# Opening of a two-model block kernel: weights brought in tile by tile, silu on one row, and a reordered softmax in layer 0

## The reference, cut to what matters

```python
c_act = jax.nn.silu(c)                              # one row of 1024
for l in range(DEPTH):                              # 2
    mod = c_act @ ada_w[l] + ada_b[l]               # 1024 x 6144
    shift_m, scale_m, gate_m, shift_f, scale_f, gate_f = split(mod, 6)
    h = rms_norm(x, g_pre_mix[l]) * (1.0 + scale_m) + shift_m
    proj = h @ w_in[l] + b_in[l]                    # 1024 x 1280
    q, k, v, u = split(proj)                        # rotary on q and k
    attn_out = sliding_window_attention_with_sinks(q, k, v, sinks[l])
    pool_out = causal_pool_mixer(u, pool_w[l], pool_scale[l])
    mix = concatenate([attn_out, pool_out]) @ w_out[l]
    x = x + gate_m * rms_norm(mix, g_post_mix[l])
    h = rms_norm(x, g_pre_ffn[l]) * (1.0 + scale_f) + shift_f
    f = (silu(h @ w_gate[l]) * (h @ w_up[l])) @ w_down[l]
    x = x + gate_f * rms_norm(f, g_post_ffn[l])
```

## Time and profile before

| what | value |
|---|---|
| runs, median of 3 | 1170.61 us (1170.38 to 1171.25) |
| profiled execution, its own time | 1170.48 us |
| span in that profile | 1168.5 us |
| PE busy | 1140.9 us, 98% of the span |
| PE weight loads | 1020.5 us, 87% |
| DVE busy | 811.5 us, 69% |
| ACT busy | 628.0 us, 54% |
| granted TensorE clock | 0.999 |
| moved by DMA | 254.04 MB, mean 217 GB/s |

### The profile page before, as it was taken

The page is one execution under the profiler, slowest core; times in us unless marked ns, Lnnn a source line. Parts: engine busy times, 40 slices in busy tenths (PEclk is TensorE's granted clock), DMA queues, the critical chain, the costliest instruction groups (busy, mean ns, idle before and its releaser), DMA issues.

```text
span 1168.5 us, 19588 instructions
## 1 busy us (share of the span) xinstructions
PE 1140.9 (98%) x7862; PEld 1020.5 (87%) x7862; DVE 811.5 (69%) x1258; ACT 628.0 (54%) x1113; POOL 29.0 (2%) x68
## 2 busy tenths in 40 slices
PE   7999999999999999999999999999999999999997
PEld 4556999999887999999899899999989889999996
DVE  6698988776998756645677667656656866766653
ACT  3077544445566544445666766445556676655443
POOL 3100000000000000000000000000000000000000
PEclk9999999999999999999999999999999999999999
DMA  9995998887445866556343546555534435555530
GB/s 361 413 378 220 355 365 329 319 334 268 189 164 198 319 231 225 210 190 238 128 181 109 180 174 217 180 183 183 187 139 156 145 132 195 196 186 194 181 109 37
DMA packets 37996, 254.04 MB, mean 217 GB/s; under 512 B 4537, under 2 KB 4881, under 8 KB 9874
## 3 DMA queue, kind: packets, MB, share of 16 engines
q1 hardware_dynamic: 35138, 243.95, 56.6%
q0 software_dynamic: 2624, 8.84, 2.1%
q10 hardware_dynamic: 144, 0.00, 0.0%
HBM read 251.69 MB, written 1.08 MB: 216 GB/s over the span
## 4 chain that ended last, share of the span: by engine, by line
PE 86%; DVE 6%; ACT 3%; DMA 3%; issue 1%; SPq 0%; DVEq 0%; ACTq 0%
PE bank L497 26%; PE bank L499 25%; PE bank L498 25%; PE bank L504 3%; DMA raw_w<-weights 2%; DVE raw_w L1641 2%; PE bank L546 2%; PE bank L595 2%; ACT gtok L1173 1%; DVE lo_w L1628 1%; DMA shared<-bias_rows 1%; PE bank L946 1%; DVE tok L1853 0%; PE bank L638 0%; PE bank L897 0%
## 5 line engine op out<-in xcount | busy, mean ns | idle before, releaser
L1628 DVE TENSOR_TENSOR lo_w<-raw_w,hi_w 128x1024 fp32r<-128x1024 f32 (+3 forms) x346 | 409.4, 1209 | 122.7 <-ACT hi_w L1168 122.3
L1168 ACT ACTIVATE hi_w<-raw_w 128x1024 fp32r<-128x1024 f32 (+3 forms) x346 | 350.6, 1040 | 103.9 <-PE bank L499 89.2
L497 PE MATMUL bank<-in_hi,lo_w 128*128 128x256 f32 x1408 | 396.0, 281 | 0.0
L499 PE MATMUL bank<-in_hi,hi_w 128*128 128x256 f32 x1408 | 392.8, 279 | 0.0
L498 PE MATMUL bank<-in_lo,hi_w 128*128 128x256 f32 x1408 | 392.8, 279 | 0.0
L497 PEld LDWEIGHTS bank<-in_hi,lo_w 128*128 128x128 f32 x1408 | 264.3, 188 | 2.6 <-issue 0.8
L498 PEld LDWEIGHTS bank<-in_lo,hi_w 128*128 128x128 f32 x1408 | 263.7, 187 | 1.9 <-issue 0.5
L499 PEld LDWEIGHTS bank<-in_hi,hi_w 128*128 128x128 f32 x1408 | 264.7, 188 | 0.0
L497 PE MATMUL bank<-hi_w,hid_lo 128*128 128x512 f32 x352 | 139.6, 396 | 0.2 <-DVE hid_lo L2116 0.2
L498 PE MATMUL bank<-lo_w,hid_hi 128*128 128x512 f32 x352 | 139.0, 395 | 0.0
L499 PE MATMUL bank<-hi_w,hid_hi 128*128 128x512 f32 x352 | 139.0, 395 | 0.0
(11 more groups left out here) (227 smaller groups left out, 1141.1 us busy)
## 6 DMA issues: line engine op xcount, KB each, us to landing
raw_w<-weights SPq DMA_DIRECT2D x213, 1024.0 KB, 4.9
ink<-ink_w SPq DMA_DIRECT2D x8, 640.0 KB, 13.9
rows<-mod_rows POOLq DMA_DIRECT2D x7, 512.0 KB, 6.9
rows<-norm_rows POOLq DMA_DIRECT2D x5, 512.0 KB, 4.9
raw_w<-weights SPq DMA_DIRECT2D x4, 512.0 KB, 8.9
ink<-whole_w SPq DMA_DIRECT2D x2, 1024.0 KB, 22.2
early_out<-whole_w SPq DMA_DIRECT2D x2, 1024.0 KB, 7.6
raw_w<-weights SPq DMA_DIRECT2D x2, 832.0 KB, 4.5
```

Of the source, the lines that this page charges most:

```text
L497: nc.tensor.matmul(o, st[1], mv[0], start=start, stop=False, **kw)
L499: return nc.tensor.matmul(o, st[0], mv[0], start=False, stop=stop, **kw)
L1168: nc.scalar.activation(hi_w[:, m % NSPLIT, cut], raw_view(unit)[:, cut], ACT.Identity).then_inc(*sig("hi_w", unit, i))
L1628: nc.vector.tensor_tensor(lo_w[:, m % NSPLIT, cut], raw_view(unit)[:, cut], hi_w[:, m % NSPLIT, cut].bitcast(F32), ALU.subtract).then_inc( ...
```

## The change

SP brings the first eight ada units (which give shift and scale) by halves of 512 KB, tile by tile: both halves of tile t, then `ink[t]`. Before, only the first two units came by halves. The vectors come ahead of them. Tiles 0, 2, 4 and 6 (the even halves) signal four new semaphores, the odd ones the ring's own. DVE goes by single tiles where it went by pairs. Silu is applied by ACT to the one row before PE spreads it, and PE's vectors and norm turns are all ahead of the first product, with the vector copy in between on DVE. The bias load waits for ada unit 5 in place of 7. In layer 0's softmax ada unit 8 moves from before the last two evacuations to after `over_sum(0)`, and every later unit one place on; ACT's `shares(3)` and `shares(4)` go ahead of `exps(4)` and `exps(5)`. Banks are taken in another order, so that the first scores don't ask for the bank of the last place.

```diff
-INK_AFTER = {("ada", 0, 0): (1,), ("ada", 0, 1): (2,), ("ada", 0, 6): (3,), ("ada", 0, 2): (4,), ("ada", 0, 7): (5,),
-             ("ada", 0, 3): (6, 7)}
+TILE_IN = (0, 1, 2, 2, 0, 0, 1, 1)
...
-                    banks(4, 5, 6, 7, 2, 3)
+                    banks(5, 6, 7, 2, 3, 4)
...
-                    banks(0, 1, 4, 0, 1, *((6, 5, 7, 4) * 4))
+                    banks(0, 1, 5, 0, 1, *((7, 6, 5, 4) * 4))
...
-            pe.wait_ge(*due("c_in", 0))
+            pe.wait_ge(*due("c_act", "row"))
             for c in range(2):
                 job = ("opening", "c", c)
                 nc.tensor.matmul(take(job)[:, :], tmp[0:1, 0:P], c_row[0:1, cols(c)], start=True, stop=True).then_inc(*sig(*job))
             pe.wait_ge(*due("const_in", 0))
-            for T in range(2):
-                turn_norm(("mix", 0), T)
             pe.wait_ge(*due("vec_in", 0))
             transposes(("opening", "vec"), [vrow[:, P * g:P * (g + 1)] for g in range(NVEC)])
+            for c in range(2):
+                for T in range(2):
+                    turn_norm(("mix", 0), T, (c,))
...
+            def tiles_in(t, name):
+                j, f = t // 2, t % 2
+                for n in (2 * j, 2 * j + 1):
+                    if n >= NRAW and f == 0:
+                        sp.wait_ge(*due("ada", UNITS[n - NRAW][0]))
+                    src = a_w[size * n:size * (n + 1)].rearrange("(p f w) -> p f w", p=P, f=2)[:, f, :]
+                    sp.dma_start(raw_w[:, n % NRAW, D * f:D * (f + 1)], src).then_inc(*sig(name(n), t, n, by=16))
+
+            for t in range(KT):
+                tiles_in(t, (lambda n: f"tile_in{TILE_IN[n]}") if t % 2 == 0 else (lambda n: f"raw_w{n % NRAW}"))
+                sp.dma_start(ink[t], a_ink[t, :, :]).then_inc(*sig(f"ink_in{t}", by=16))
...
             angles()
+            pool.wait_ge(*due("ada", ("ada", 0, 5)))
+            load(bias, a_bias[0:1, :], 1280, "bias_in", 0)
             pool.wait_ge(*due("ada", ("ada", 0, 7)))
-            load(bias, a_bias[0:1, :], 1280, "bias_in", 0)
...
+            sc.preload_act_table_set("silu_and_others")
+
+            sc.wait_ge(*due("c_in", 0))
+            nc.scalar.activation(c_row[0:1, :], c_row[0:1, :], ACT.Silu).then_inc(*sig("c_act", "row"))
             sc.preload_act_table_set("natural_log_exp_and_others")
...
                 nc.scalar.activation(r, r, ACT.Exp, scale=-0.5).then_inc(*sig("rstd", N, 1))
-                sc.preload_act_table_set("silu_and_others")
 
                 sc.wait_ge(*due("opening", "c", 1))
                 for c in range(2):
-                    nc.scalar.activation(c_row[:, cols(c)], ps(("opening", "c", c))[:, :], ACT.Silu).then_inc(*sig("c_act", c, frees=("opening", "c", c)))
+                    copy(("opening", "c", c), c_row[:, cols(c)], ps(("opening", "c", c))[:, :], "c_act", c)
...
                     exps(3)
                     probT_in(0)
+                    shares(3)
                     exps(4)
-                    shares(3)
                     probT_in(1)
+                    shares(4)
                     exps(5)
-                    shares(4)
                     probT_in(2)
...
                 for T in range(2):
-                    norm(N, T)
-                ve.wait_ge(*due("c_act", 1))
-                ada_tile(0, 4, 0)
-                ada_tile(0, 0, 0)
+                    norm(N, T, (0,))
                 ve.wait_ge(*due("opening", "vec"))
                 nc.vector.tensor_copy(vcol[:, :], ps(("opening", "vec"))[:, 0:NVEC * P]).then_inc(*sig("vcol", 0, frees=("opening", "vec")))
+                for T in range(2):
+                    norm(N, T, (1,))
+                ve.wait_ge(*due("c_act", 1))
...
+                for t in range(KT):
+                    j, f = t // 2, t % 2
+                    ada_tile(0, 4 + j, f)
+                    last = ada_tile(0, j, f)
...
-                    ada(0, 8)
                     evacuate(0, 0, 2)
                     evacuate(0, 1, 2)
...
                     over_sum(0)
-                    ada(0, 9)
+                    ada(0, 8)
                     over_sum(1)
                     scored(2)
-                    ada(0, 10)
+                    ada(0, 9)
                     over_sum(2)
...
-                    for n in (18, 19, 12, 13, 14, 15):
+                    for n in (17, 18, 19, 12, 13, 14, 15):
```

More of the change, by code:

```diff
@@ L1031, in _ @@
                     sp.wait_ge(*due(*(("ada", old) if old[0] == "ada" else ("lo_w", old, 1))))
-                part, src = ((raw_w[:, n, D:2 * D], tiles[n][:, 1, :]) if n < 2 else
-                             (raw_view(unit), a_w[off:off + P * kt * n_cols].rearrange("(p w) -> p w", p=P)))
-                sp.dma_start(part, src).then_inc(*sig(f"raw_w{n % NRAW}", unit, by=16))
+                sp.dma_start(raw_view(unit), a_w[off:off + P * kt * n_cols].rearrange("(p w) -> p w", p=P)).then_inc(
+                    *sig(f"raw_w{n % NRAW}", unit, by=16))
                 off += P * kt * n_cols
@@ L1038, in _ @@
                     sp.dma_start(whole[u].rearrange("p t c -> p (t c)"), a_whole[u, :, :]).then_inc(*sig(f"whole_in{u}", by=16))
-                for kk in INK_AFTER.get(unit, ()):
-                    sp.dma_start(ink[kk], a_ink[kk, :, :]).then_inc(*sig(f"ink_in{kk}", by=16))
             for T in range(2):
@@ L1703, in scale, with norm @@
                     nc.vector.tensor_tensor(scaled[:, cols(c)], x[:, T, cols(c)], rows[:, 1, cols(c)], ALU.mult).then_inc(*sig("scaled", N, T, c))
-            def norm(N, T):
+            def norm(N, T, parts=(0, 1)):
                 ve.wait_ge(*due("rstd", N, 1 if N == ("mix", 0) else T))
                 r = tok_rstd[:, T, 1:2]
-                for c in range(2):
+                for c in parts:
                     dst = final[:, T, cols(c)] if N[0] == "final" else normed[:, cols(c)]
@@ L1835, in started @@
                         ve.wait_ge(*due("ada", ("ada", 0, j)))
                     ve.wait_ge(*due("vcol", 0))
-                    mod_column(0, "shift", 0, 0, a, b, shift[:, a:b])
-                    step(mod_column(0, "scale", 0, 8, a, b, scale[:, a:b]))
-                    for t in tiles:
-                        for T in range(2):
-                            ve.wait_ge(*due("turned", T, t // 4))
-                        nc.vector.tensor_scalar(raw[:, t, :], raw[:, t, :], scale[:, t:t + 1], shift[:, t:t + 1], ALU.mult, ALU.add).then_inc(
-                            *sig("scaled0", t))
+                    mod_column(0, "shift", 0, 0, t, t + 1, shift[:, t:t + 1])
@@ L1845, in in_job @@
+                    step(mod_column(0, "scale", 0, 8, t, t + 1, scale[:, t:t + 1]))
+                    for T in range(2):
+                        ve.wait_ge(*due("turned", T, t // 4))
+                    nc.vector.tensor_scalar(raw[:, t, :], raw[:, t, :], scale[:, t:t + 1], shift[:, t:t + 1], ALU.mult, ALU.add).then_inc(*sig("scaled0", t))
             def in_job(L, T, c):
@@ L2001, in attention_mixed @@
                 if L == 2:
-                    ve.wait_ge(*due("const_late", 0))
+                    ve.wait_ge(*due("const_in", 2))
                 ve.wait_ge(*due("crow_in", L))
```

51 lines of the change are left out of this document (23 added, 28 removed).

## The result

The changed kernel takes 1173.03 us at the median of 17 runs (1170.98 to 1174.64), the kernel before 1170.83 (1170.04 to 1171.51, 17 runs on the same chip). The ratio is 1.0018, with a 95% interval of 1.0012 to 1.0025: it is slower, by about 2.1 us. The forecast was 1170.3 in a range of 1168.0 to 1172.2; the time lies 0.8 above that range. The profiled execution took 1171.84 with a span of 1170.0, so it is one of the shorter ones, and what it shows is less than the whole loss.

The account below looks back on a forecast made before the run. The prediction took the boundary after layer 0's attention, waiting for the landing of `gu` 0 behind a full transfer queue, as the bound. It summed -0.7 (boundary) and +0.5 (landing) to -0.2 us: 1170.3, range 1168.0 to 1172.2.

Parts of the forecast that it names:

- the scores wait for no evacuation: Layer 0's attention: the first scores' wait of 1.67 us for DVE's last evacuation goes; they start at about 53.7.
- a wait for modcol ahead of the second row: PE, near 81 us: being early, it waits 1 to 2 us for the second modcol row it spreads.
- the shares worth nothing: Layer 0's softmax: PE's wait of 1.41 us at 74.14 goes, but PE then waits for modcol instead.
- the landing: Transfer of `gu` 0, landing at 92.9 before: 0.5 us lost, bounds 0 to 1.9, because later units are issued later.
- the upper bound: Transfer queue: each unit lands 5.5 us after its issue, unit 15 at 77.3 against 75.4, so 1.9 us lost.
- The gain of DVE in front is given back by the unit moved: DVE after `over_sum(5)`: there at 75.6 for 77.57, but at 77.9 with the seventh unit; last needed modcol at 92.0 to 92.3.
- 0.7 gained: Boundary after layer 0's attention: PE's turn of the norm ends at 102.65 us in place of 103.35.
- The turn: PE's turn of the boundary's norm: first half forecast to start at 101.35 us, before at 102.31.
- the norm's wait: DVE at the boundary: the norm's wait of 0.53 us shrinks by some 0.35, to 100.65.
- both waits of TensorE (near 41, and near 81): PE waits 2 to 3 us for `raw` late in the tiles and 1 to 2 us for modcol.
- Rival C: First transfer window: halves go at 377 in place of 420 GB/s, all lands 3.5 later; +2.8 us, 1173.3; chance 0.11.
- the prediction's own sign of being wrong: Boundary: `gu` 0 lands below 91 or above 95.9 us, or the boundary no longer waits for it.

Follow-up runs that it names:

- e7: The kernel before with only the shares ahead of the exps and the two new lists of banks: 1169.36 us, ratio 0.9985.
- e5: The kernel before with all of the softmax edits (unit 8 moved, shares, banks) and the old opening: 1171.01 us, ratio 1.0003.
- e1: The changed kernel with ada unit 8 put back ahead of the last two evacuations: 1171.35 us, ratio 1.0006.
- e8: The kernel before with the new opening alone; unit 8, shares and banks as before: 1173.32 us, ratio 1.0013.
- e11: The changed kernel with unit 8 put back and unread TensorE products ahead of tiles 6 and 7: 1169.94 us, ratio 0.9985.
- e13: The kernel before with the new opening alone and unread TensorE products ahead of tiles 6 and 7: 1171.59 us, ratio 1.0005.
- e9: The changed kernel, unit 8 left moved, with unread TensorE products ahead of tiles 6 and 7: 1173.10 us, ratio 1.0017.
- e15: The changed kernel with unit 8 put back, unread products, and the load of `whole[1]` issued behind `gu` 0: 1172.57 us, ratio 1.0014.

## Why the prediction was wrong

**Right.** Table load, tiles, bias and halves cost next to nothing in this profile's rows (414 GB/s from 12.6 to 43.2 where it was 420, first product at 14.05, products through at 54.2 where 53.7 was forecast); the scores wait for no evacuation; `scored(0)` at 55.43 for 54.9; unit 12 issued at 60.5 for 59.8; a wait for modcol ahead of the second row, 2.26 for "1 to 2"; the shares worth nothing.

**The step that failed first** is *the landing*, "I take 0.5 lost, near the row of 0.6". In the profiled execution it was 1.0 for `gu` 0 and 2.0 for the unit ahead of it, and 2.4 for `gu` 0 in the kernel with the unread products, against its twin with unit 8 ahead, where the bound was 1.9. Unit 15, issued at 72.0, landed at 77.7, behind even the 77.3 of the upper bound. The sum took the lead of units 12 and 13 alone. What counts is the ring: with unit 8 late, every slot up to `gu` 0's comes free a place late, and the queue misses up to 1.2 MB from 58 to 66 (407 against 262 GB/s). Most of those bytes don't come back, since the rest of the way to `gu` 0 is at full load: from 58 to 93 it is 397 against 371 GB/s in e7 and e5, 0.9 MB.

**Its twin** is the sentence "The gain of DVE in front is given back by the unit moved". The forecast booked unit 8's move as neutral against the wait that the banks remove, and so a gain in sum. The runs price the two apart: banks -1.4 us; unit 8 +1.65 on the old opening, and on the new one +3.2 with the unread products and, from the ratios of the changed kernel and e1, +1.4 without. So the other term of the sum, "0.7 gained" at the boundary, fails with it. The turn was forecast at 101.35 and came at 103.16; the norm's wait didn't shrink (0.54 for 0.53), and TensorE wasn't early. The right comparison was not with the kernel before, but with the banks alone: the banks had already taken the first scores off the evacuation's bank, so that unit 8 had no need to move.

**The term that was missing** is the granted clock. The prediction forecast both waits of TensorE (near 41, and near 81) and put nothing behind them. Where the clock fell behind them, the work took longer: 14 products in 6.23 for 4.54, 64 products in 6.77 for 5.06. The fall seems to come in most executions, not in all (by the two groups of e8, 8 of 11; only one execution of each kernel was profiled). By e1 against e11 (2.1 thousandths), and e8 against e13 (0.8), it is worth 1 to 2.5 us, which is the 1.7 and what it delays. Rival C had the right sign for another reason: the halves didn't slow the queue. And the prediction's own sign of being wrong, `gu` 0 below 91 or above 95.9, didn't show: it landed at 93.9, and VectorE still waited for it. The turn was set by TensorE, of which the sign took no account.

**The sum**, from the parts alone: opening +1.5 (1.0013), banks -1.4 (0.9988), shares +0.1 (1.0001), unit 8 +1.65, together +1.85, for the 2.1 measured. Each term has some 1 us of uncertainty (by its median the opening alone would be +2.6), and e5's profile has a fall in it too, so the agreement is in part luck. What stays open: why the clock falls in one execution and not in the next at waits of the same length (2.10 with a fall in e1's profile, 2.09 without in e8's; 2.26 with one in the changed kernel's, 2.26 without in e9's), and whether unit 8 costs more on the new opening (3.2) than on the old one (1.65). The starts of the turn speak for scatter: they differ by 2.4 in the one pair and by 2.2 in the other. Unread products could also act through something other than the clock; the profiles show no other effect of theirs.

## What to carry to other kernels

Where a ring of buffers feeds a full queue, a consumer moved one place back delays every release behind it, not one; count the bytes missing in the window, since a queue that runs dry for a moment doesn't catch up. When an edit takes away a wait, price the companion edits one by one: here the banks alone give 1.4 us, and the whole change loses 2.1. And a wait that "costs nothing" because TensorE is early isn't free when the clock falls behind it: give it something to do, or let it come later.

## What the hardware showed

The granted clock went from 1.00 to 0.50, from the level of 2.4 GHz to that of 1.2, behind waits of TensorE of 2.10 (e1), 2.26 (the changed kernel) and 2.59 us (e15), and the work behind each took 1.7 us longer. Where TensorE is early anyway it costs little: the kernel before with banks and shares has such a fall at 15.5 in its profile, behind the wait ahead of the first product, and its scores start at 54.14, against 53.94 with the banks alone and no fall. The Trainium skill, page "TensorE: Matmul & The Clock Gate", section "HAM oscillation — how this bites in real kernels", describes this pattern, products that wait for a transfer and start again at half clock. These runs agree with the pattern, though of the three waits only the one of 2.59 is for a transfer and the others are for VectorE. But it isn't sure to come: the opening alone has a wait of 2.09 in its profile and no fall, e9 one of 2.26 and none.
